# Second mixer's attention on one core: a fourth buffer of weights, reciprocals and gate products for two units at once, and every copy of transposed weights halved between VectorE and ScalarE

## The reference

```
q, k_c, v_c, k_s, v_s, k_w, v_w, z, g_logit = split(h @ w_in)   # 16 heads of 64, 4 groups of keys
o_cmp = softmax(q . k_cmp) @ v_cmp                               # compressed keys, done before
q_r, k_s, k_w = rope_partial(q), rope_partial(k_s), rope_partial(k_w)
o_sel = softmax(mask(q_r . k_s * scale)) @ v_s    # top 16 of 8 blocks: all of them, so causal
o_win = softmax(mask(q_r . k_w * scale)) @ v_w    # window of 512: causal as well
gate = sigmoid(g_logit + b_gate)                  # 3 per head and token
o = gate0 * o_cmp + gate1 * o_sel + gate2 * o_win
return (o * silu(z)) @ w_out
```

## Time and profile before

| what | us |
|---|---|
| median of 3 runs | 1899.04 (1898.32 to 1901.15) |
| the profiled execution | 1899.72 |
| its span, first to last instruction | 1898.0 |
| PE busy in the span | 1824.1 |
| DVE busy | 1095.2 |
| ACT busy | 675.3 |
| POOL busy | 308.9 |

### The profile page before, as it was taken

The page is one execution under the profiler, slowest core; times in us unless marked ns, Lnnn a source line. Parts: engine busy times, 40 slices in busy tenths (PEclk is TensorE's granted clock), DMA queues, the critical chain, the costliest instruction groups (busy, mean ns, idle before and its releaser), DMA issues. The chain is left out here.

```text
span 1898.0 us, 36850 instructions
## 1 busy us (share of the span) xinstructions
PE 1824.1 (96%) x15870; PEld 1484.7 (78%) x15870; DVE 1095.2 (58%) x1644; ACT 675.3 (36%) x1100; POOL 308.9 (16%) x292
## 2 busy tenths in 40 slices
PE   8999999999999788999999899999999999999997
PEld 6877757688888567778888669888878888888886
DVE  4664354553257788444366887778574635354545
ACT  4334332332223577442222374433233322122342
POOL 4210011130002565320021240000001000000011
PEclk9999999999999899999999999999999999999998
DMA  5334323142223010134421100002042322322221
GB/s 191 103 111 134 136 83 133 45 190 101 90 74 111 35 37 12 49 109 138 137 102 56 48 2 4 4 3 70 4 178 92 104 104 89 111 89 89 78 100 45
DMA packets 42848, 160.87 MB, mean 85 GB/s; under 512 B 5312, under 2 KB 14528, under 8 KB 28096
## 3 DMA queue, kind: packets, MB, share of 16 engines
q1 hardware_dynamic: 28480, 143.84, 22.1%
q10 hardware_dynamic: 14208, 14.68, 2.2%
HBM read 140.42 MB, written 16.78 MB: 83 GB/s over the span
## 5 line engine op out<-in xcount | busy, mean ns | idle before, releaser
L257 DVE TENSOR_TENSOR wlo<-raw,whi 128x2048 fp32r<-128x2048 f32 (+2 forms) x113 | 251.0, 2221 | 179.2 <-ACT whi L248 178.8
L248 ACT ACTIVATE whi<-raw 128x2048 fp32r<-128x2048 f32 (+2 forms) x113 | 209.0, 1850 | 320.8 <-PE ps L283 161.4
L281 PE MATMUL ps<-act_hi,whi 128*128 128x512 f32 x616 | 243.1, 395 | 0.0
L301 PE MATMUL ps<-act_lo,whi 128*128 128x512 f32 x632 | 242.7, 393 | 0.0
L283 PE MATMUL ps<-act_hi,wlo 128*128 128x512 f32 x616 | 240.6, 391 | 0.0
L282 PE MATMUL ps<-act_lo,whi 128*128 128x512 f32 x616 | 240.5, 390 | 0.0
L300 PE MATMUL ps<-act_hi,whi 128*128 128x512 f32 x592 | 236.4, 399 | 0.0
L305 PE MATMUL ps<-act_hi,wlo 128*128 128x512 f32 x632 | 156.5, 389 | 0.0
L301 PEld LDWEIGHTS ps<-act_lo,whi 128*128 128x128 f32 x632 | 120.2, 190 | 25.9 <-issue 1.2
L305 PEld LDWEIGHTS ps<-act_hi,wlo 128*128 128x128 f32 x632 | 118.6, 188 | 24.7
L300 PEld LDWEIGHTS ps<-act_hi,whi 128*128 128x128 f32 x592 | 111.6, 188 | 32.5 <-issue 8.2
(11 more groups left out here) (550 smaller groups left out, 3474.7 us busy)
## 6 DMA issues: line engine op xcount, KB each, us to landing
raw<-stream_in SPq DMA_DIRECT2D x107, 1024.0 KB, 4.9
v_scratch<-v_out ACTq DMA_DIRECT2D x16, 256.0 KB, 3.5
z_scratch<-zt ACTq DMA_DIRECT2D x16, 256.0 KB, 2.9
mlh_v<-v_scratch SPq DMA_DIRECT2D x4, 1024.0 KB, 4.8
mlh_z<-z_scratch SPq DMA_DIRECT2D x16, 256.0 KB, 2.6
cmp_w<-cmp_w_in SPq DMA_DIRECT2D x2, 2048.0 KB, 11.3
z_scratch<-in_zt ACTq DMA_DIRECT2D x16, 256.0 KB, 3.2
mix_g<-z_scratch SPq DMA_DIRECT2D x16, 256.0 KB, 6.6
```

Source lines behind the costliest of these rows:

```text
L248: act.activation(k.whi[b % 2][:, 0:n], k.raw[b % RAW_SLOTS][:, 0:n], ACT.Copy).then_inc(k.hi_done, 1)
L257: dve.tensor_tensor(k.wlo[b % 2][:, 0:n], k.raw[b % RAW_SLOTS][:, 0:n], k.whi[b % 2][:, 0:n].bitcast(F32), ALU.subtract).then_inc(k.lo_don ...
L281: pe.matmul(bank, hi, x_hi, start=(x == 0), stop=False)
L301: pe.matmul(bank, hi, x_lo, start=False, stop=False)
```

## The change

- Before the attention: query tiles 2 and 3 are no longer rounded and split by ACT and DVE in the projection (`None` in `high_at`), but by POOL at the very start of the attention (`high`, `low` for t = 2, 3). Their high parts move to a slot of raw weights, and the wait for the transposed values goes.
- `att_p` has four buffers instead of three (`DEEP`), and all that follows the scaling stands one step later: transposes, copies, y. The burst moves from even to odd steps.
- Reciprocal and gate product are done once for two units, on four elements, in even steps, behind y where both stand in one step. `w_done` counts pairs.
- `COPIES = TT`: bank 4 of the widest units is now copied by DVE as well, and ACT copies bank 5 alone.

```diff
-    high_at = (17, 18, 23, 23, 24, 24, 25, 25)
+    high_at = (17, 18, 23, 23, None, 24, None, 25)
...
+    DEEP, COPIES = 4, TT
+    p = k.region("att_p", [P, DEEP, 2, S], F32, 16)
...
+            for t in (2, 3):
+                high(t)
+                low(t)
             for m in range(U):
                 L = length(m)
-                pool.wait_ge(s["w_done"], m + 1)
-                pool.tensor_scalar(p[:, m % 3, 0, 0:L], p[:, m % 3, 0, 0:L], sm(32, m)[:, 0:1], None, ALU.mult) \
+                pool.wait_ge(s["w_done"], m // 2 + 1)
+                pool.tensor_scalar(p[:, m % DEEP, 0, 0:L], p[:, m % DEEP, 0, 0:L], sm(32, m)[:, 0:1], None, ALU.mult) \
...
-            for n in range(U + 3):
+            for n in range(U + DEEP):
                 if n + 1 < U:
                     scores(n + 1)
-                if 2 <= n < U + 2:
-                    m = n - 2
+                if DEEP - 1 <= n < U + DEEP - 1:
+                    m = n - DEEP + 1
...
-                if n >= 4 and n % 2 == 0:
-                    c = n // 2 - 2
+                if n > DEEP and n % 2:
+                    c = (n - DEEP) // 2
...
-                if n >= 7 and n % 4 == 3:
-                    u = (n - 7) // 4
+                if n >= 8 and n % 4 == 0:
+                    u = (n - 8) // 4
...
-                if 1 <= n <= U:
-                    m = n - 1
-                    dve.wait_ge(s["exp_done"], 2 * m + 2)
-                    steps.then_wait(dve, dve.reciprocal(sm(24, m), sm(8, m)))
...
+                if 2 <= n <= U and n % 2 == 0:
+                    c = n // 2 - 1
+                    dve.wait_ge(s["exp_done"], 2 * n)
+                    steps.then_wait(dve, dve.reciprocal(pair(24, c), pair(8, c)))
...
+                    for m in (n - 2, n - 1):
+                        L = length(m)
+                        dve.tensor_scalar(p[:, m % DEEP, 1, 0:L], p[:, m % DEEP, 1, 0:L], sm(32, m)[:, 1:2], None, ALU.mult) \
+                            .then_inc(s["scaled1"], 1)
-                if 2 <= n < U + 2 and units[n - 2][1] < TT - 1:
-                    m = n - 2
+                if DEEP - 1 <= n < U + DEEP - 1 and units[n - DEEP + 1][1] < COPIES:
+                    m = n - DEEP + 1
```

More of the change, by code:

```diff
@@ L1687, in score_low @@
                 whole, hi, lo = parts(n)
-                dve.wait_ge(s["score_hi"], n + 1)
+                dve.wait_ge(s["score_hi"], 1 + sum(at is not None for at in high_at[:n]))
                 dve.tensor_tensor(lo, whole, hi.bitcast(F32), ALU.subtract)
@@ L1766, in _ @@
                 for n in range(8):
-                    if high_at[n] == t - 1:
+                    if high_at[n] is not None and high_at[n] == t - 1:
                         score_low(n)
@@ L1803, in sm, with pair @@
         return k.small[:, base + 2 * (n % 4):base + 2 * (n % 4) + 2]
+    def pair(base, c):
+        return k.small[:, base + 4 * (c % 2):base + 4 * (c % 2) + 4]
     def copied(eng, m):
         eng.wait_ge(s["pt1"], m + 1)
-        own = sum(i < TT - 1 for _, i, _ in units[:m + 1])
+        own = sum(i < COPIES for _, i, _ in units[:m + 1])
         if own:
@@ L1891, in _ @@
                                 rows, at = rows_half(half), (TT * e + j) * P // 2
-                                last = pe.transpose(k.ps[:, 4 + half, at:at + P // 2], p[rows, m % 3, e, j * P:(j + 1) * P],
+                                last = pe.transpose(k.ps[:, 4 + half, at:at + P // 2], p[rows, m % DEEP, e, j * P:(j + 1) * P],
                                                     k.const("ident")[rows, rows])
                     last.then_inc(s["tr_mm"], 1)
-                if n >= 4 and n % 2 == 0:
-                    c = n // 2 - 2
+                if n > DEEP and n % 2:
+                    c = (n - DEEP) // 2
                     u = c // 2
@@ L1925, in high @@
                     act.activation(k.act_hi[:, 4 * gp + 2 * e + x, :], y[:, x, e, :], ACT.Copy).then_inc(s["y_hi"], 1)
-            for n in range(U + 2):
+            for n in range(U + DEEP - 1):
                 if n < U:
@@ L1944, in _ @@
                         act.wait_ge(s["pv_mm"], m // 2 - 1)
-                    if units[m][1] == TT - 1:
+                    if units[m][1] == TT - 1 >= COPIES:
                         out = pt[m // 2 % 2][:, m % 2].rearrange("p e (j h q) -> p h (e j) q", j=TT, h=2)
@@ L1949, in _ @@
                     else:
+                        if units[m][1] >= COPIES:
+                            out, src = turned(m, 0)
+                            act.activation(out, src, ACT.Copy)
                         out, src = turned(m, 1)
@@ L1968, in low @@
                     dve.tensor_tensor(k.act_lo[:, tile, :], y[:, x, e, :], k.act_hi[:, tile, :].bitcast(F32), ALU.subtract)                         .then_inc(s["y_lo"], 1)
-            for n in range(U + 4):
+            for n in range(U + DEEP + 1):
                 if n < U:
```

41 lines of the change are left out of this document (18 added, 23 removed).

## The result

| | time, median | range of the runs |
| --- | --- | --- |
| before, 15 runs beside the change | 1899.59 us | 1896.67 to 1903.1 |
| the change, 15 runs | 1904.11 us | 1900.05 to 1907.98 |

The ratio is **1.0017, 95% interval 1.001 to 1.0024**: by it the change is some 3.2 us slower (the two medians lie 4.5 us apart), inside the 0.2% that I called no change, but on the other side of it. The profiled execution took 1901.81 us (span 1900.1).

A forecast was written before the change was run, and what follows sets the result against it. TensorE, busy 96% of the span, was taken as the bound, with quarters a ring of short waits. Quarters -3.2, start +1.0, end +0.2, projection -0.6 sum to -2.6 us: 1896.4 us, range 1889 to 1904.

The forecast's parts named there:

- The first two blocks: Second attention quarter, hand schedule: first block loses 0.6 us with DVE full of copies, second wins 1.9.
- The start: Attention's start: POOL's 3.8 us of splits hidden, but unit 0 scaled later; +1.0 us, bounds 0 and 2.
- rival 3: Wide blocks get longer and thinner for TensorE, so its clock drops; 2.4 us more, 1898.8; chance 0.09.
- the projection: Before the attention: two DVE subtractions and two ACT roundings go; -0.6 us, bounds 0 and -1.7.
- the third and the fourth lose 0.1 and 0.3: Last two blocks of the second quarter: POOL's scalings after y end 0.8 to 0.9 us late for TensorE's transposes.
- rival 2: Slower: y, waiting for the burst, holds back the pair's weights sixteen times; 9.6 us more, 1906; chance 0.17.
- DVE's load is then 28.0 us, unchanged: DVE per quarter: 28.1 us, less 2.9 for reciprocals and gate products, plus 2.8 for added copies.
- 0.05 us per pair for the meeting: DVE's second scaling running inside POOL's first costs 0.05 us per pair, 1.6 us in all at worst.
- Rival 4: DVE's second scaling waits for POOL's by the port lock; about 1.0 us, 32 times: 1927; chance 0.04.
- the vanished waits of maxima: In the quarters, the maximum waiting behind the burst has no weights queued behind it; called the real gain.
- The end: Attention's tail: last units scaled as a pair by POOL, first one 0.7 us later; +0.2 us, bounds 0 and 1.
- the sign of a wrong forecast: The stage from first scores to last y, about 150 us, moving by more than 4 us.

The follow-up runs named there:

- number 3: The kernel before with only the rounding and splitting of query tiles 2 and 3 moved to POOL at the attention's start; ratio 0.9997 to the kernel before.
- number 9: The change with y moved behind the pair's weights and scalings in DVE's order, run in two batches; ratios 0.9989 and 0.9993 to the kernel before.
- number 6: The change with DVE's second scaling of a pair one step later, reciprocals and products still by pairs; ratio 1.0008 to the kernel before.
- number 10: The change with y behind the pair's weights and DVE's second scaling one step later; ratio 0.9977 to the kernel before.
- number 2: The change with POOL starting a pair's scalings only after DVE has ended both of its own; ratio 1.0077 to the kernel before.
- number 1: The change with only the halved copies taken back, ACT copying 1,024 columns in one instruction; ratio 1.0034 to the kernel before.
- number 11: The change with unit weights and the widest units' copies whole on ACT, so the fourth buffer alone; ratio 0.9994 to the kernel before.
- number 7: The kernel before with only the widest units' copies halved between DVE and ACT, three buffers and old order; ratio 1.0028 to the kernel before.
- number 4: The change with only the pairing undone: reciprocal, product and scaling unit by unit, four buffers, halved copies; ratio 0.9986 to the kernel before.

## Why the prediction was wrong, step by step

**Right.** The load that was taken away and added: ACT 7.0 us less for 6.8, copies 0.69 and 0.60 us, reciprocals 0.17. The first two blocks (8.9 and 9.8 by hand, 9.05 and 9.99 measured). The start: the pair's weights come 6.2 us after the first maximum, where 6 was forecast, and POOL's splits end before. No fall of the clock in the wide blocks of the later quarters, so rival 3 is out.

**A term that was too small: the projection.** Forecast -0.6 us with a bound of -1.7; the last eviction came 1.47 us earlier. Both effects came: the key's subtraction, 1.77 us beside POOL's multiplication, now stands 0.4 us earlier, at 611.82, and takes 0.68. By itself the move is worth nothing that the ratio shows (number 3).

**The step that failed: "the third and the fourth lose 0.1 and 0.3", y's place ahead of the pair's weights.** That is rival 2's mechanism, which had 0.17. My schedule charged y through POOL alone, whose scalings would end 0.8 to 0.9 us after TensorE wants to transpose, and no term in it is DVE's own idle time before y. Measured, the two blocks lost 0.6 and 0.5 us in the second quarter, and moving y gives 0.5 and 0.5 back (number 9). Over the four quarters that is 4.1 us by the steps of the traces, some 5 by the ratio: more than all of the 3.2 us that the change lost. The cost came through DVE's list, not through POOL: DVE waits 0.71 to 0.75 us for the burst, and with y in front the pair's weights, the copy and the next maximum all wait with it; in the wide blocks, where y does not wait, its place costs nothing. Rival 2's price was 9.6 us, so half of it came true. Its sign, a wait of over 1 us for POOL after every y, came in the third blocks (1.13 to 1.15 us); it was 0.94 in the fourth and 0.62 to 0.82 in the second.

**A second step that failed: "DVE's load is then 28.0 us, unchanged", with 0.05 us per pair for the meeting.** I took that 0.05 from one row, a DVE scaling that began 1.6 us into POOL's, 0.26 us before its end. In the change the second scaling starts 0.34 us into POOL's and ends 0.83 us after the first (two in 1.32, the first 0.49). Over the widths the mean durations exceed those before by 0.21, 0.16, 0.11 and 0.05 us, 16 scalings each: 8.5 us in all, 2.1 a quarter, for the 1.6 us in all that I had as the worst; DVE's busy time in the stage grew by 6.6 us. What the meeting costs in time is not shown by itself. Moving the second scaling, which avoids it and also spreads the load, is worth about 2 us: 1.7 from number 6, 2.3 to 3 from number 10 against number 9, each within intervals of about 2 us.

Rival 4, scalings that wait for POOL's end, did not happen in the change: the second scaling ended at 671.36 in the pair that began at 670.04, and POOL's first, begun at 670.10 and 1.85 us long, at 671.95. The Trainium skill ("SBUF — State Buffer", section "SBUF: two separate sides") has GpSimd's instructions under an exclusive lock with VectorE's of two ports or of two inputs from SBUF: the first to start holds the ports, the other blocks. The rows of number 2 disagree for two scalings, since there both engines lose 0.2 us each on average by meeting and neither waits out the other. For a two-input instruction on POOL the rows agree, and more closely than I read them: the subtraction at 612.19 did not end with POOL's multiplication, at 613.42, but 0.54 us after it.

**A reason that was wrong although its sign came.** I credited the vanished waits of maxima to the order (no weights behind the burst). With whole copies in the new order these waits are back, 15.8 us in all for 7.9 (number 1) and 14.3 for 7.1 (number 11), and with halved copies in the old order (number 7) they are gone, 6.9 for 14.2: they went with the halving, in every order. In number 7 they went and the kernel was slower all the same, so their going is no gain by itself. That ACT's copy of 1.03 us holds the next transposes, and these the scores behind them, is my reading of it, in line with the earlier trace rows.

**And the parts do not add.** Halving costs 5.3 us (0.0028) with three buffers; with four it wins 1.5, inside the intervals, and with four and pairs 3.2. Four buffers alone give 0.6 us, inside their interval. I had treated them as one net term. The third quarter (37.84 us for 35.78 before) is the largest loss in the change's profile and partly open: moving the subtractions out of the full steps gives 0.9 us back in one profile, y's place 0.9, and no run tells the rest. The end took 6.2 us from the last maximum to the last y for 5.5, inside its bound of 1. The stage as a whole grew by 3.9 us, just under the 4 that I had named as the sign of a wrong forecast.

The sum as the runs have it: four buffers, halved copies and the queries' split -2.7 us (close to the -2.6 for the whole by luck, since that counted pairing in), and pairing +5.9; together +3.2. Within pairing, y's place costs some 5 us and the second scaling's place about 2; what pairing itself saves, 2.9 us of DVE a quarter, is worth about -1.7 us, and only once both are taken away (0.9977 against 0.9986, 0.9975 against 0.9984; the intervals overlap, so the sign itself is not certain).

## What to carry to other kernels

When work is gathered for two units, look at what stands **ahead** of it on its engine in that step, and at what stands behind. An engine that runs its list in order loses the whole wait of an instruction at the head, and everything behind it moves with it; the same instruction costs nothing in a step where it does not wait. Before the gathered version is given up, move the waiting instruction behind it and spread what need not be gathered. Compare two traces step by step before naming a cause: the wait that the profile names on one engine can shrink without being what was won. And price a meeting of two engines from a row in which the second instruction starts near the beginning of the first, not near its end.

## What the runs showed of the hardware

A scaling of 128 x 512 f32 in place takes DVE 0.48 us and POOL 1.58 us when they are apart (number 2). Started together, DVE keeps 0.49 and POOL takes 1.85 to 1.87 (number 4). A second DVE scaling, started 0.34 us after POOL's, ends 0.83 us after the first, 0.6 us before POOL's does (the change). Each is slowed by part of the other's time, and neither is shut out.

A two-input instruction on POOL is another matter. A subtraction on DVE that started 0.38 us into POOL's two-input multiplication took 1.77 us for 0.68. A DVE scaling of 128 columns, 0.28 us by itself, took 1.36 beside POOL's two-input subtraction in number 10, and ended 0.08 us after it:

```profile
665.57 1.36 DVE L2002 TENSOR_SCALAR att_p<-att_p,small 128x128 f32<-128x128 f32 x1
665.58 1.27 POOL L1832 TENSOR_TENSOR nsa_q_lo<-nsa_q,act_lo 128x512 fp32r<-128x512 f32 x1
```
